# Neighbourhood attention: five PSUM banks used in turn by scores and transposes, with a new order on TensorE and ScalarE

## What is computed

```
s_nb = einsum('bqhd,bkhd->bhqk', qb, kb) * scale + bias      # keys of the grid window
s_cx = einsum('bqhd,bkhd->bhqk', qb, k_ctx) * scale          # 256 context keys
p    = softmax(concatenate([s_nb, s_cx], -1))
out  = einsum('bhqk,bkhd->bqhd', p[..., :nk], vb) + einsum('bhqk,bkhd->bqhd', p[..., nk:], v_ctx)
```

## Time and profile before

| | |
|---|---|
| median of three runs | 1363.12 us |
| profiled execution, its own time | 1366.11 us |
| its span, first to last instruction | 1364.3 us |
| TensorE busy | 1052.2 us (77%) |
| VectorE busy | 477.1 us (35%) |
| ScalarE busy | 283.2 us (21%) |
| GpSimd busy | 36.3 us (3%) |
| bytes moved by DMA | 486.96 MB, mean 357 GB/s |

### The profile page before, as it was taken

One profiled execution on the slowest core, in us unless ns is written; L12 is line 12 of the kernel. 1 busy time (PEld: TensorE's weight loads), 2 busy tenths in 40 slices (PEclk: granted clock), 3 DMA queues, 4 the chain that ended last, 5 costly groups with the idle time before them and its releaser, 6 DMA issues.

```text
span 1364.3 us, 16777 instructions
## 1 busy us (share of the span) xinstructions
PE 1052.2 (77%) x7282; PEld 620.5 (45%) x7282; DVE 477.1 (35%) x895; ACT 283.2 (21%) x502; POOL 36.3 (3%) x69
## 2 busy tenths in 40 slices
PE   8999999999999985585675756677585675756676
PEld 7987986799978732131231312313131231313223
DVE  5967877887896311011010101101011010101113
ACT  6536665754265200000000000000000000000002
POOL 0001100000000000000000000000000000000000
PEclk9999999999999998787778878777777778878779
DMA  9655168344436999999999999999999999999996
GB/s 381 250 208 230 70 260 365 131 155 185 185 124 278 398 428 433 434 436 434 426 432 433 437 430 429 434 431 436 431 429 429 436 431 431 430 434 434 428 424 263
DMA packets 21138, 486.96 MB, mean 357 GB/s; under 512 B 2536, under 2 KB 3081, under 8 KB 4937
## 3 DMA queue, kind: packets, MB, share of 16 engines
q1 hardware_dynamic: 20200, 484.31, 84.2%
q10 hardware_dynamic: 864, 1.57, 0.3%
HBM read 484.83 MB, written 1.05 MB: 356 GB/s over the span
## 4 chain that ended last, share of the span: by engine, by line
PE 49%; DMA 43%; DVE 6%; issue 1%; ACT 1%; SPq 0%; DVEq 0%; ACTq 0%
PE ps L281 47%; DMA places<-in_experts 43%; DVE xT L1803 2%; DVE R L1771 1%; DVE R L1767 1%; PE ps L1443 0%; DMA ring<-in_pieces 0%; PE ps L1815 0%; DVE ring_r L335 0%; DVE hT_r L528 0%; DVE hT L511 0%; PE ps L1088 0%; PE ps L1161 0%; DVE hT_r L520 0%; DVE ring_r L349 0%
## 5 line engine op out<-in xcount | busy, mean ns | idle before, releaser
L281 PE MATMUL ps<-places,R 128*32 128x512 f32 (+2 forms) x3168 | 458.8, 740 | 269.2 <-DMA places<-in_experts 267.2
L281 PEld LDWEIGHTS ps<-places,R 128*32 128x32 f32 x3168 | 111.8, 134 | 595.4 <-DMA places<-in_experts 308.8
L1764 DVE SCALAR_TENSOR_TENSOR R<-R,ps 128x512 f32<-128x512 f32 x16 | 11.0, 686 | 305.7 <-ACT R L1759 305.7
L281 PE MATMUL ps<-hT_r,ring_r 128*128 128x256 f32 x400 | 113.6, 284 | 0.0
L281 PE MATMUL ps<-U_r,ring_r 128*128 128x256 f32 x480 | 107.7, 284 | 0.4 <-DVE hT_r L528 0.3
L335 DVE TENSOR_TENSOR ring_r<-ring,ring_r 128x2048 fp32r<-128x2048 f32 (+1 forms) x44 | 98.7, 2275 | 21.3 <-ACT ring_r L329 21.3
L1767 DVE SCALAR_TENSOR_TENSOR R<-R,ps 128x512 f32<-128x512 f32 x16 | 11.0, 688 | 229.7 <-PE ps L281 229.7
L281 PE MATMUL ps<-late_r,ring_r 128*128 128x256 f32 x448 | 84.5, 286 | 0.9 <-DVE U_r L540 0.7
L329 ACT ACTIVATE ring_r<-ring 128x2048 fp32r<-128x2048 f32 (+1 forms) x44 | 81.5, 1896 | 6.8 <-DMA ring<-in_pieces 4.8
L281 PEld LDWEIGHTS ps<-U_r,ring_r 128*128 128x128 f32 x480 | 82.1, 192 | 1.2 <-DVE hT_r L528 1.0
L281 PEld LDWEIGHTS ps<-hT_r,ring_r 128*128 128x128 f32 x400 | 77.2, 193 | 0.7 <-issue 0.5
(11 more groups left out here) (365 smaller groups left out, 1080.3 us busy)
## 6 DMA issues: line engine op xcount, KB each, us to landing
places<-in_experts SPq DMA_DIRECT2D x54, 6144.0 KB, 49.4
places<-in_experts SPq DMA_DIRECT2D x29, 2048.0 KB, 17.3
ring<-in_pieces SPq DMA_DIRECT2D x20, 2048.0 KB, 8.5
ring<-in_wmodt SPq DMA_DIRECT2D x8, 2048.0 KB, 8.2
ring<-in_wmodk SPq DMA_DIRECT2D x4, 2048.0 KB, 9.3
ring<-in_pieces SPq DMA_DIRECT2D x2, 1024.0 KB, 6.9
places<-in_experts SPq DMA_DIRECT2D x2, 1024.0 KB, 33.1
ring<-in_pieces SPq DMA_DIRECT2D x1, 1792.0 KB, 12.6
```

Source lines behind the costliest of these rows:

```text
L281: mm = lambda e, o, l, r, st, sp_=True, sk=False: e.matmul(o, l, r, start=st, stop=sp_, skip_group_check=sk)
L1764: e.scalar_tensor_tensor(h, h, 1.0, bank[2 * (ex % 2)][:, :], ALU.add, ALU.mult).then_inc(s["me_h2"], 1)
```

## The change

Scores and transposes of unit u now share one bank, `bank[u % 5]`: T(u) writes over the scores of u, which the exponential has read by then. T(u) no longer waits for a copy. S(i) waits instead until the transposed unit 2i-4 has been copied out of the bank (`na_tc >= 2i-3`). At iteration i, TensorE now issues T(2i-4), O(i-3), T(2i-3) and only then S(i); ScalarE issues C(2i-4), E of unit 2i-2, C(2i-3), E of unit 2i-1, so that the exponentials stand one iteration later than before. VectorE's order is the same except for two low parts of weights: chunk 42 moves from iteration 3 to 5 and chunk 43 from iteration 4 to 6. Two waits for exponentials ahead of `pe_proj` 45 and 46 go, since the transposes that now stand earlier imply them, and three calls of `pe_idle` with a count of 0 go. No instruction of work is added or removed.

```diff
-    na_b = lambda u: bank[u % 3]
+    na_b = lambda u: bank[u % 5]
...
-        if i >= 1:
-            e.wait_ge(s["na_e"], 2 * i - 1)
+        if i >= 2:
+            e.wait_ge(s["na_tc"], 2 * i - 3)
...
-    def pe_na_t(e, i):
-        for u in (2 * i, 2 * i + 1):
-            b = bank[3 + u % 2]
-            e.wait_ge(s["na_p"], 2 * u + 2)
-            if u >= 2:
-                e.wait_ge(s["na_tc"], u - 1)
-            for j in range(4):
-                k = e.transpose(b[:, j * 128:(j + 1) * 128], na_pb(u)[:, j * 128:(j + 1) * 128], c_("ident"))
-            k.then_inc(s["na_t"], 1)
+    def pe_na_t(e, u):
+        e.wait_ge(s["na_p"], 2 * u + 2)
+        for j in range(4):
+            k = e.transpose(na_b(u)[:, j * 128:(j + 1) * 128], na_pb(u)[:, j * 128:(j + 1) * 128], c_("ident"))
+        k.then_inc(s["na_t"], 1)
...
@@ TensorE's loop
+            if 0 <= i - 2 < 8:
+                pe_na_t(e, 2 * i - 4)
+            if 0 <= i - 3 < 8:
+                pe_na_o(e, i - 3)
+            if 0 <= i - 2 < 8:
+                pe_na_t(e, 2 * i - 3)
             if i < 8:
                 pe_na_s(e, i)
             if i == 0:
                 pe_proj(e, 44, cs=(4, 5, 6, 7), first=False, at=5, **X2)
-            if 0 <= i - 3 < 8:
-                pe_na_o(e, i - 3)
             if i == 9:
-                pe_na_t(e, 7)
                 pe_router_b(e)
...
-            if 0 <= i - 2 < 7:
-                pe_na_t(e, i - 2)
...
@@ ScalarE's loop
-            if i == 7:
-                act_na_t(e, 5)
-            if i < 8:
-                act_na_exp(e, i)
+            if 0 <= i - 2 < 8:
+                act_na_t(e, 2 * i - 4)
+            if 0 <= i - 1 < 8:
+                act_na_exp(e, 2 * i - 2)
+            if 0 <= i - 2 < 8:
+                act_na_t(e, 2 * i - 3)
+            if 0 <= i - 1 < 8:
+                act_na_exp(e, 2 * i - 1)
...
-            if 0 <= i - 2 < 8 and i != 7:
-                act_na_t(e, i - 2)
...
@@ VectorE's loop
             if i == 3:
                 conv(42)
                 dve_cf_norm(e)
-                conv(43)
             if i == 4:
                 dve_cf_inv(e)
-                conv(44)
+            if i in (5, 6):
+                conv(38 + i)
```

More of the change, by code:

```diff
@@ L1420, in dve_na_max, with act_na_exp @@
             e.tensor_reduce(s4(u, 1), na_b(u)[:, :], AX.X, ALU.max, negate=True).then_inc(s["na_mx"], 1)
-    def act_na_exp(e, i):
-        for u in (2 * i, 2 * i + 1):
[L1424 to L1427, removed]
+    def act_na_exp(e, u):
+        e.wait_ge(s["na_mx"], u + 1)
+        if u >= 4:
+            e.wait_ge(s["na_t"], u - 3)
+        e.activation(na_pb(u), na_b(u)[:, :], ACT.Exp, bias=s4(u, 1), accum_out=s4(u, 2)).then_inc(s["na_e"], 1)
     def dve_na_norm(e, i):
@@ L1434, in dve_na_norm, with act_na_t @@
             e.tensor_scalar(na_pb(u), na_pb(u), s4(u, 3), None, ALU.mult).then_inc(s["na_p"], 1)
-    def pe_na_t(e, i):
-        for u in (2 * i, 2 * i + 1):
-            b = bank[3 + u % 2]
-            e.wait_ge(s["na_p"], 2 * u + 2)
-            if u >= 2:
-                e.wait_ge(s["na_tc"], u - 1)
-            for j in range(4):
-                k = e.transpose(b[:, j * 128:(j + 1) * 128], na_pb(u)[:, j * 128:(j + 1) * 128], c_("ident"))
-            k.then_inc(s["na_t"], 1)
[L1446 to L1451, removed]
+    def pe_na_t(e, u):
[3 more added lines that the diff above has]
+        k.then_inc(s["na_t"], 1)
+    def act_na_t(e, u):
+        e.wait_ge(s["na_t"], u + 1)
+        if u >= 4:
+            e.wait_ge(s["na_o"], (u - 4) // 2 + 1)
+        e.activation(na_pt(u), na_b(u)[:, :], ACT.Copy).then_inc(s["na_tc"], 1)
     def pe_na_o(e, i):
@@ L2136, in pe_program @@
             if i == 2:
-                pe_idle(e, 0)
                 pe_hy_f(e, 0)
@@ L2142, in pe_program @@
                 pe_hy_f(e, 1)
-            if i == 3:
-                pe_idle(e, 0)
+            if 0 <= i - 2 < 8:
[4 more added lines that the diff above has]
+                pe_na_t(e, 2 * i - 3)
             if i < 8:
@@ L2148, in pe_program @@
                 pe_proj(e, 44, cs=(4, 5, 6, 7), first=False, at=5, **X2)
-            if 0 <= i - 3 < 8:
-                pe_na_o(e, i - 3)
             if i == 9:
-                pe_na_t(e, 7)
                 pe_router_b(e)
-                e.wait_ge(s["na_e"], 14)
                 pe_proj(e, 45, ready=("sp_lo", lambda c: (19, 20, 17, 18)[c - 4]), cs=(6, 7, 4, 5), last=False, **XN)
             if i == 10:
-                e.wait_ge(s["na_e"], 15)
                 pe_proj(e, 46, cs=(4, 5, 6, 7), last=False, **XN)
@@ L2162, in pe_program @@
                 pe_cf_var(e)
-            if 0 <= i - 2 < 7:
-                pe_na_t(e, i - 2)
             if i == 8:
                 e.wait_ge(s["hy_m"], 8)
-                pe_idle(e, 0, 6)
                 pe_hy_i(e, 1)
```

## The result

The changed kernel took 1379.62 us (median of four runs, 1377.51 to 1381.25) where the kernel before took 1363.63 us beside it: a ratio of 1.0115, 95% interval 1.0103 to 1.0128. It is 16.0 us slower. The forecast was 1374.9 us with a range up to 1379.0. The direction and the mechanism of the waits were right, and the time lies 0.6 us above the range. In a later comparison, beside the first three experiments, it took 1378.97 us against 1364.53 us, ratio 1.0109 (1.0095 to 1.0123), 14.9 us slower.

What follows compares the result with a forecast made beforehand. The expert weight stream fills two thirds of the span, and the end moves with TensorE's arrival at expert 0. Waits of 10.1 us plus 1.7 of clock, +11.8 us, gave 1374.9 us, range 1369.8 to 1379.0.

Steps and rivals of the forecast that it cites:

- 1.9 us was all there was to win: Attention loop, 378.5 to 428.2 us: TensorE's waits there, all a better order could win, are 1.9 us.
- The end of the kernel moves with TensorE's arrival at expert 0: Start of the expert stage: TensorE, not the weight stream, is late by about 1.5 us; delay shows one for one.
- The dip at 470 to 475 us: Weight stream at fetch 12: it waits for TensorE to have used place 0, losing some 1.5 us.
- The sum of 12.05 us: Attention loop: TensorE's waits in six places, 0.3 to 3.8 us each, 12.05 us in place of 1.9.
- the old places of the low parts: VectorE, iterations 4 and 5: two low parts left where they were would add up to 2.2 us.
- one short fall's worth, 1.7 us: TensorE's clock in the attention loop: one short fall behind the long waits, costing 1.7 us.
- The bounds (0 to 6.6): TensorE's clock in the loop: from no fall to two falls of 6.6 us at half speed, 6.6 us together.
- The rule of the Trainium skill: Attention loop: stepping through PSUM banks leaves TensorE short idles and its clock swings; by it, the second rival's sum.
- The stream: Start of expert weights: fetch 2 goes out 8.6 us later, near 428.2, fetch 4 some 10 us later.
- Adds nothing: Start of expert weights: the late stream, fetch 2 by 8.6 us, is no more than TensorE's own delay, adding nothing.
- The clock swings for the whole loop: Rival, attention loop: a third of the remaining wall time at 1.2 GHz, +6.6 us, 1379.8 us; chance 0.13.
- The other three: Rivals: the stream sets the end, 1370.2 us, chance 0.12; faster, 1361.2 us, 0.04; no change, 1363 us, 0.05.

Runs made afterwards that it cites:

- the first three experiments: The changed kernel again, 1378.97 us; with 13 idle matmuls ahead of T(2) and of T(12), 1376.45 us; with VectorE's scaling ahead of the maxima, 1370.83 us.
- the filler: The changed kernel with 13 idle matmuls ahead of T(2) and of T(12), where TensorE only waits: 1376.45 us, 11.5 us above the kernel before.
- the scaling first: The changed kernel with VectorE's scaling N(i-1) ahead of the maxima M(i) in iterations 2, 3, 4, 6 and 7: 1370.83 us, 6.7 us above the kernel before.

## Why the prediction was wrong, point by point

- *What bounds the kernel.* Right that the expert stream does. That 1.9 us was all there was to win stands as read from the rows; no run won any of it. "The end of the kernel moves with TensorE's arrival at expert 0", one for one, came out where the loop made the stream late as well, which the prediction did not name as its condition; for TensorE alone there is a slack of about 2 us first (1.1 us for 3.2, 11.6 for 13.5). The dip at 470 to 475 us was read as TensorE late by 1.5 us, with nothing to spare; but 3.2 us more there deepened it by 1.8 only. Why those 1.4 us cost nothing no run settles.
- *The waits.* The sum of 12.05 us came out as 12.7, each of the six within 0.15 us but one. T(12) waited 4.38 and not 3.8: chunk 43 ends 0.7 us behind S(7), where I had costed it at "nothing, or 0.3 us". The sentence on the old places of the low parts ("up to 2.2 us") was wrong; they cost nothing there.
- *The clock.* **This is the step that failed.** I took "one short fall's worth, 1.7 us". There were two falls, one behind each long wait, of 6.8 us each in the first profile (3.4 and 6.8 us in the second), and together they took 4.1 to 4.9 us of TensorE's time and 2.5 to 3.4 us of the end. The bounds (0 to 6.6) held it; the choice inside them didn't, and the range ended at 1379.0, below the 1379.8 that the upper bound for the clock gives. The reason for the low choice, that the slowed work lay partly off the path, did not hold either. It lay on it: behind the first wait O(0), T(3) and S(3), each in line for VectorE's next turn, and with the clock held up the loop was 4.1 to 4.9 us shorter. Both waits were longer than the 2.97 us of the earlier trace rows behind which there had been a fall, so the rows asked for two falls.
- *The rule of the Trainium skill*, that a kernel which cycles through PSUM banks leaves TensorE short idles and its clock swings (the Trainium skill, page "TensorE: Matmul & The Clock Gate", section "A second HAM failure mode: psum-queue depth-cycling"): the trace agrees in part. The clock swung in the changed loop, mean 0.89, and stayed up in the kernel before, which cycles too. What told the two apart was the length of single waits: in this loop, falls behind 2.19, 2.67, 3.68 and 4.38 us, none behind 1.98 us and less. That isn't the whole story, though: the early fall of the earlier trace rows, at 11.7 us in the kernel before, has no single wait of more than 1.48 us ahead of it, but three in a row (0.46, 1.48 and 0.45 us). The longest of them, and the same work at half clock behind the fall (0.55 us in place of 0.35):

```profile
9.55 0.35 PE L281 MATMUL ps<-R_r,ring_r 128*128 128x256 f32 x1 [1.48 <-DVE hT_r L520]
...
12.34 0.55 PE L281 MATMUL ps<-R_r,ring_r 128*128 128x256 f32 x1 [0.38 <-DVE hT_r L520]
```

None of the other profiles has a fall there; their longest wait between 5 and 15 us is 1.24 us. So a few waits of 1.5 us and less can go with a fall too, as that section has it. This is read from one profile, and no run was made on this place; it may be part of why that execution came late to the loop.

- *The stream.* Fetch 2 was 11.4 to 12.2 us late and not 8.6, fetch 4 15.3 to 16.1 and not "some 10", mostly by the clock (with the filler they were 9.8 and 11.2 us late). Between them the stream ran dry: 4 MB last 9.7 us at 432 GB/s, fetch 4 came 12.8 behind fetch 2. That hole (0 GB/s at 442 to 443) was not in the sum. "Adds nothing" was right only against a sum that counted TensorE one for one: by the runs with TensorE alone late, its delay would have cost some 2 us less than it is long, an estimated 13 to 14 us, and the changed kernel lost 14.9 (13.0 to 16.8) and 16.0. The late stream took that slack away. How much of it is the hole and how much the late start is not shown.
- *The sum.* 10.1 + 1.7 = 11.8 forecast. Measured for TensorE: 11.1 of waits (12.74 less 1.68) and 4.1 to 4.9 of clock, of the 15.3 to 16.1 us by which the loop grew; at the end 14.9 to 16.0. Of the 4.7 us between 1374.9 and 1379.62, the waits are 1.0, the clock is 2.4 to 3.2 (or 0.8 to 1.7 by what the filler won at the end), and 0.5 is the kernel before, which ran at 1363.63 and not 1363.12 beside it.
- *The rivals.* "The clock swings for the whole loop" named the right term, +6.6 us and 1379.8 us, and was the nearest in time, but by some luck: the clock fell only behind the long waits and took 4.1 to 4.9 us, and the rest of that time was longer waits and a slower yardstick. The other three did not happen.

## What to carry to other kernels

When two engines hand work to and fro in fixed orders, count what stands between "A needs B" and "B needs A" on each: here TensorE's O and T were the cover for VectorE's turn, and moving them ahead of the scores cost more than every wait for a bank had. Price such a wait from the rows where the same turn ran covered; that was exact here to 0.15 us in five places of six. Then price what TensorE does behind it at half clock, once for each wait at least as long as the shortest single wait behind which the nearest rows show a fall. Let the range reach up to all of these falls at the longest duration in the rows. And if the wait can't be avoided, try to fill it with idle matmuls.

## What was not expected of the hardware

- Idle matmuls in two waits won 2.5 to 3.4 us of 1379, though the transposes behind the waits started no sooner after the scores.
- The clock fell behind a single wait of 2.19 us (S(3) with the scaling first) and 2.67 us, and did not behind 1.98, 1.87 and 1.48 us; in another stage it fell with no single wait above 1.48 us ahead.
- A scaling of 128 x 512 on VectorE takes 0.49 us alone and 1.53 us when a GpSimd multiply of 1.27 us starts just ahead of it: the sum of both less 0.23 us. Moving it off that multiply gave the microsecond back.
- Each arrival at the expert stream had some 2 us to spare by itself: TensorE 3.2 us late cost 1.1 (-0.1 to 2.3), and fetch 2 8.3 us late cost 6.0 (4.2 to 7.6). With both late there was nothing to spare: 7.4 us late cost 6.7, 9.4 cost 9.8, 16.1 cost 16.0.
